# A head's convolution tile accumulated in PSUM between the scores' mask and the mean's sum; early tiles take one GLU group more; gates multiplied in ahead of the variance

## The reference

```python
h = rms_norm(x, norm_g);  z = h @ w_in
(c_glu, c_gate, r_q, r_k, r_v, r_gate, a_q, ...) = split(z)
# convolution branch: 1024 channels, 31 taps along the sequence
v = a * sigmoid(b)                       # a, b = halves of c_glu
y = conv_general_dilated(v, dw, depthwise, width 31) + db
y = silu(layer_norm(y)) * silu(c_gate)
# retention branch: 4 heads, q/k of 256, v of 512
q, k = rotary(q), rotary(k)
o = (q k^T * decay) v                    # both directions
o = (o - mean(o)) * rsqrt(var(o) + EPS)  # over the head's 512 values
y_ret = (o * silu(r_gate)) @ w_ret_out
...
x = x + (g0 * y_conv + g1 * y_ret + g2 * y_attn) @ w_out
```

## Time and profile before

| what | value |
|---|---|
| median of 3 runs | 3453.9 us (3451.58 to 3454.66) |
| the profiled execution | 3454.71 us, its span 3452.9 us |
| TensorE busy | 3243.9 us, 94% of the span |
| DVE, POOL, ACT busy | 1696.8, 1330.2, 1130.9 us |
| mean granted TensorE clock | 0.971 |

### The profile page before, as it was taken

One profiled execution on the slowest core, in us unless ns is written; L12 is line 12 of the kernel. 1 busy time (PEld: TensorE's weight loads), 2 busy tenths in 40 slices (PEclk: granted clock), 3 DMA queues, 4 the chain that ended last, 5 costly groups with the idle time before them and its releaser, 6 DMA issues.

```text
span 3452.9 us, 42695 instructions
## 1 busy us (share of the span) xinstructions
PE 3243.9 (94%) x14040; PEld 2532.5 (73%) x14040; DVE 1696.8 (49%) x2508; ACT 1130.9 (33%) x1623; POOL 1330.2 (39%) x966
## 2 busy tenths in 40 slices
PE   7989999899999898999989999998999999999998
PEld 5866776667888686776766778885787787688885
DVE  4945854765343376745857544245654051341113
ACT  3232232255242222332323653223544332222222
POOL 3433443311555343433433134452334344244542
PEclk9999999999999999999999999999999999999999
DMA  4211222210322322211221022222112223222222
GB/s 150 92 62 61 73 73 66 69 37 25 116 98 92 106 92 73 68 67 61 73 74 55 30 81 92 97 98 79 64 64 73 91 81 102 67 90 97 94 97 73
DMA packets 73172, 272.07 MB, mean 79 GB/s; under 512 B 8128, under 2 KB 9152, under 8 KB 72384
## 3 DMA queue, kind: packets, MB, share of 16 engines
q1 hardware_dynamic: 69984, 252.74, 22.2%
q10 hardware_dynamic: 3072, 17.82, 1.4%
HBM read 264.24 MB, written 8.39 MB: 79 GB/s over the span
## 4 chain that ended last, share of the span: by engine, by line
PE 76%; DVE 11%; DVEq 9%; issue 2%; ACT 1%; DMA 0%; ACTq 0%; POOL 0%; SPq 0%; POOLq 0%
PE gem L296 18%; PE gem L298 18%; PE gem L297 18%; DVEq L1269 3%; PE xp L380 3%; PE xp L536 2%; DVE xp L1233 2%; PE xp L372 2%; DVEq L1235 2%; PE gem L499 2%; DVE zlo L1207 1%; PE gem L633 1%; PE gem L634 1%; PE gem L635 1%; PE xp L506 1%
## 5 line engine op out<-in xcount | busy, mean ns | idle before, releaser
L266 POOL TENSOR_TENSOR wlo<-raw,whi 128x512 fp32r<-128x512 f32 x956 | 1329.4, 1412 | 2078.6 <-ACT whi L774 2078.1
L296 PE MATMUL gem<-hhi,whi 128*128 128x512 f32 x2320 | 935.0, 403 | 4.5 <-POOL wlo L266 3.7
L298 PE MATMUL gem<-hhi,wlo 128*128 128x512 f32 x2320 | 905.1, 390 | 0.0
L297 PE MATMUL gem<-hlo,whi 128*128 128x512 f32 x2320 | 904.1, 390 | 0.0
L774 ACT ACTIVATE whi<-raw 128x1024 fp32r<-128x1024 f32 x478 | 504.4, 1056 | 753.5 <-PE gem L298 651.7
L296 PEld LDWEIGHTS gem<-hhi,whi 128*128 128x128 f32 x2320 | 436.3, 188 | 109.1 <-issue 17.5
L297 PEld LDWEIGHTS gem<-hlo,whi 128*128 128x128 f32 x2320 | 436.5, 188 | 104.5 <-issue 16.3
L298 PEld LDWEIGHTS gem<-hhi,wlo 128*128 128x128 f32 x2320 | 436.1, 188 | 92.1
L296 PE MATMUL gem<-zhi,whi 128*128 128x512 f32 x1008 | 405.6, 402 | 77.0 <-DVE yr L1337 59.9
L297 PE MATMUL gem<-zlo,whi 128*128 128x512 f32 x1008 | 401.9, 399 | 0.0
L298 PE MATMUL gem<-zhi,wlo 128*128 128x512 f32 x1008 | 401.0, 398 | 0.0
(11 more groups left out here) (228 smaller groups left out, 3383.8 us busy)
## 6 DMA issues: line engine op xcount, KB each, us to landing
raw<-in_slabs SPq DMA_DIRECT2D x478, 512.0 KB, 3.4
U<-xsave ACTq DMA_DIRECT2D x2, 2048.0 KB, 7.9
xsave<-U ACTq DMA_DIRECT2D x2, 2048.0 KB, 7.5
U<-in_x ACTq DMA_DIRECT2D x1, 2048.0 KB, 9.5
out_y<-yr SPq DMA_DIRECT2D x8, 256.0 KB, 2.0
tab<-in_tab_ret ACTq DMA_DIRECT2D x2, 512.0 KB, 8.0
tab<-in_tab_att ACTq DMA_DIRECT2D x2, 512.0 KB, 3.6
tab<-in_tab_hg ACTq DMA_DIRECT2D x1, 512.0 KB, 8.0
```

Of the source, the lines that this page charges most:

```text
L266: part = pool.tensor_tensor(wlo[:, k % 4, c], raw[:, k % 2, c], whi[:, k % 4, c].bitcast(f32), O.subtract)
L296: pe.matmul(o, wh, hi, start=(n == 0), stop=False)
L297: pe.matmul(o, wh, lo, start=False, stop=False)
L298: mm = pe.matmul(o, wl, hi, start=False, stop=(n == len(terms) - 1))
```

## The change

- The head's convolution tile accumulates in the `xp` banks 2 and 3, from which the scores have just been read. Its first 27 taps (`HEAD_CUT`) stand right behind `mask_scores`, ahead of the `sum4` that waits for the head's output; the last 4 and the final sum stand behind the `sum4` of the squares. Nothing of it is left in `add_out`.
- `pv` has two banks instead of four (`v % 2`): its third and fourth product wait until ACT has read the first and the second (`o_ready`). The transposes into banks 2 and 3 wait for the end of the convolution (`conv_done`).
- The gate's products (`gate_products`) are taken out of `gated` and stand behind the `sum4` of the squares. `gated` splits two tiles at a time.
- The early convolution has 8 pieces of 12 taps, one behind each GLU product from the first on, instead of 6 of 13; the last tap writes to SBUF directly, which saves a copy. The `memset` of `yr` moves ahead of the GLU.

```diff
-CUTS = (17, 21, 25, 28, TAPS)
-EARLY, EARLY_GLU, EARLY_PIECE = 4, 6, 13
+EARLY, EARLY_GLU, EARLY_PIECE = 4, 8, 12
+HEAD_CUT = 27
...
                 def pv(hd, v):
                     if v == 0:
                         pe.wait_ge(st_ready, L * 16 + hd * 4 + 4)
+                    if v >= 2:
+                        pe.wait_ge(o_ready, L * 16 + hd * 4 + (v - 1))
                     for j in range(4):
-                        mm = pe.matmul(xp[:, v, :], VT[:, j, v * P:(v + 1) * P], ST[:, j, :],
+                        mm = pe.matmul(xp[:, v % 2, :], VT[:, j, v * P:(v + 1) * P], ST[:, j, :],
...
                     for k in range(4, 8):
                         hslab(Gn, k, un)
+                        if k == 5:
+                            pe.wait_ge(conv_done, L * 4 + hd + 1)
...
+                dve.memset(yr[:, :, :], 0.0)
                 for it in range(4):
...
-                        if it:
-                            n = (it * 2 + k // 2 - 2) * EARLY_PIECE
-                            early_conv(n, n + EARLY_PIECE)
+                        n = (it * 2 + k // 2) * EARLY_PIECE
+                        early_conv(n, n + EARLY_PIECE)
                 early_conv(EARLY_GLU * EARLY_PIECE, EARLY * TAPS)
-                dve.memset(yr[:, :, :], 0.0)
...
                     for n in range(first, end):
-                        a, v = TT[:, n % 2, :], cv[:, i, n:n + T]
+                        acc, v, w = xp[:, 2 + n % 2, :], cv[:, i, n:n + T], DW[:, n:n + 1]
                         if n < 2:
-                            ts(a, v, DW[:, n:n + 1], None, O.mult)
+                            ts(acc, v, w, None, O.mult)
                         else:
-                            stt(a, v, DW[:, n:n + 1], a, O.mult, O.add)
+                            stt(acc if n < TAPS - 1 else TT[:, 0, :], v, w, acc, O.mult, O.add)
...
                     mask_scores(hd)
+                    conv(hd + EARLY, 0, HEAD_CUT)
                     sum4(OT, o_ready, L * 16 + hd * 4 + 4, osum)
                     center(hd)
                     sum4(ST, osq, L * 16 + hd * 4 + 4, ossq)
-                    dve.drain()
+                    gate_products(hd)
+                    conv(hd + EARLY, HEAD_CUT, TAPS)
                     dve.wait_ge(ovar, L * 4 + hd + 1)
                     rope(G + 1, u + 1, 0)
                     gated(hd)
                     rope(G + 1, u + 1, 1)
                     dve.drain()
-                    conv(hd + EARLY, 0, CUTS[0])
-                    add_out(G + 3, u + 3, hd + EARLY)
+                    add_out(G + 3, u + 3)
```

More of the change, by code:

```diff
@@ L195, in build @@
         vt_done, vt_ready, score_done, st_ready = (sem(n) for n in ("vt_done", "vt_ready", "score_done", "st_ready"))
-        pv_done, o_ready = sem("pv_done"), sem("o_ready")
+        pv_done, o_ready, conv_done = sem("pv_done"), sem("o_ready"), sem("conv_done")
         osum, omean, ocent, osq, ossq, ovar, orstd = (sem(n) for n in (
@@ L438, in layer @@
                 hslab(G + 1, 3, u + 1)
+                pe.wait_ge(conv_done, L * 4 + 4)
                 for v in range(2):
@@ L851, in o_read @@
                     act.wait_ge(pv_done, L * 16 + hd * 4 + (v + 1))
-                    act.activation(OT[:, v, :], xp[:, v, :], A.Copy).then_inc(o_ready, 1)
+                    act.activation(OT[:, v, :], xp[:, v % 2, :], A.Copy).then_inc(o_ready, 1)
                 def gates(G, hd):
@@ L1232, in early_conv @@
                             else:
-                                stt(acc, v, w, acc, O.mult, O.add)
+                                stt(acc if n < TAPS - 1 else TT[:, 0, :], v, w, acc, O.mult, O.add)
                             if n % 2:
@@ L1237, in early_conv @@
                             dve.drain()
-                            dve.tensor_copy(TT[:, 0, :], xp[:, 0, :])
-                            dve.drain()
                             stt(cv[:, i, PAD:PAD + T], xp[:, 1, :], vec[:, C_CB + i:C_CB + i + 1], TT[:, 0, :], O.add, O.add)
+                dve.memset(yr[:, :, :], 0.0)
                 for it in range(4):
@@ L1248, in layer, with conv @@
                             .then_inc(evac[k], 1)
-                        if it:
-                            n = (it * 2 + k // 2 - 2) * EARLY_PIECE
-                            early_conv(n, n + EARLY_PIECE)
+                        n = (it * 2 + k // 2) * EARLY_PIECE
+                        early_conv(n, n + EARLY_PIECE)
                 early_conv(EARLY_GLU * EARLY_PIECE, EARLY * TAPS)
-                dve.memset(yr[:, :, :], 0.0)
-                def conv(i, first=0, end=TAPS):
+                def conv(i, first, end):
+                    dve.drain()
                     if first == 0:
-                        dve.drain()
                         dve.tensor_copy(DW[:, 0:TAPS], vec[:, bass.ds(i * TAPS + C_DW, TAPS)])
@@ L1271, in conv @@
                         dve.drain()
-                        stt(cv[:, i, PAD:PAD + T], TT[:, 0, :], DW[:, TAPS:TAPS + 1], TT[:, 1, :], O.add, O.add)
+                        stt(cv[:, i, PAD:PAD + T], xp[:, 3, :], DW[:, TAPS:TAPS + 1], TT[:, 0, :], O.add, O.add)\
+                            .then_inc(conv_done, 1)
                         dve.drain()
@@ L1316, in center, with gate_products @@
                         stt(OT[:, v, :], xp[:, 0, :], -1.0 / T, OT[:, v, :], O.mult, O.add).then_inc(ocent, 1)
+                def gate_products(hd):
+                    for v in range(4):
+                        tt(OT[:, v, :], OT[:, v, :], SG[:, v, :], O.mult)
                 def gated(hd):
@@ L1321, in gated, with add_out @@
                     dve.wait_ge(orstd, L * 4 + hd + 1)
[L1322 to L1331, removed]
+                    for v in range(0, 4, 2):
+                        for w in (v, v + 1):
+                            tt(OT[:, w, :], OT[:, w, :], RS, O.mult)
+                        dve.drain()
+                        for w in (v, v + 1):
+                            dve.tensor_copy(zhi[:, w, :], OT[:, w, :])
+                        dve.drain()
+                        for w in (v, v + 1):
+                            tt(zlo[:, w, :], OT[:, w, :], zhi[:, w, :].bitcast(f32), O.subtract).then_inc(z_ready, 1)
+                def add_out(G, u):
                     for k in range(4):
@@ L1337, in add_out @@
                             tt(yr[:, o, :], gem[:, b, :], yr[:, o, :], O.add).then_inc(evac[b], 1)
-                        if i is not None:
-                            conv(i, CUTS[k], CUTS[k + 1])
                 G, u = g0 + QKV0[0], u0 + QKV0[1]
@@ L1368, in layer @@
                 mask_scores(3)
+                conv(EARLY + 3, 0, HEAD_CUT)
                 sum4(OT, o_ready, L * 16 + 16, osum)
@@ L1371, in layer @@
                 sum4(ST, osq, L * 16 + 16, ossq)
+                gate_products(3)
+                conv(EARLY + 3, HEAD_CUT, TAPS)
                 gated(3)
@@ L1383, in layer @@
                 square(0)
-                conv(EARLY + 3, 0, CUTS[0])
-                add_out(G + 2, u + 2, EARLY + 3)
+                add_out(G + 2, u + 2)
                 def a_norm_rope(n):
```

## The result

The changed kernel takes 3379.68 us (median of 4 runs, 3376.34 to 3380.46) against 3454.28 for the kernel before on the same chip: a ratio of 0.9783, 95% interval 0.9766 to 0.9800. That is 74.6 us less, where 69.4 were forecast. The profiled execution took 3380.46 us with a span of 3378.7, so 74.2 of the 3452.9 before are gone; its mean granted clock is 0.980.

What follows compares the result with a forecast made beforehand. TensorE, busy 94% of the span, was taken as the bound. The terms 78.7 + 27.3 + 5.0 - 22.4 - 19.2 = 69.4 us gained gave 3454.7 - 69.4 = 3385.3, stated as 3385 us, range 3356 to 3412.

Steps and rivals of the forecast that it cites:

- `add_out`, 78.7: TensorE's eight waits for `add_out`, in four heads of two layers, all go: 59.9 us plus 18.8 of low clock.
- The early tiles, 27.3: Early convolution tiles finish in time, so both first-head rope waits go: 22.9 us plus 4.4 of low clock.
- The convolution fits: In each head, 27 taps with weight copies take 23.4 us in 29.0 us of room and cost nothing.
- My dearer price: Taps at 1.002 us, as with SBUF accumulators: a head's 27 would take 28 us and still fit.
- The new `pv` waits, 22.4: The third `pv` waits for ACT's read behind a table load: 2.8 us in each of eight heads, 22.4 lost.
- The fourth rival: ACT's `pv` read comes 1.4 us later behind the table load; eight heads lose 11 us: 3398 us. Chance 0.02.
- The clock behind them, 19.2: Lower granted clock behind the eight new `pv` waits: 2.4 us a head, 19.2 lost, bounds nothing and 4.4 each.
- Head 3, 5.0: TensorE's wait for `zlo` in head 3 shrinks: 2.5 us gained per layer, 5 in all, bounds nothing and 14.
- this rival: The convolution doesn't fit at 1.76 us a tap; TensorE waits 19.4 us at each mean: 3559 us. Chance 0.04.
- my 8.7: Wait in us per head, at the mean, at which the 69.4 us gain would be used up.
- The rope wait: Rival: early tiles finish late and TensorE waits for the first head's rope again, 27.3 us: 3412. Chance 0.05.
- the stall: Rival: with `add_out` prompt, a 3.7 us wait for POOL's weights comes in each head, 30 us: 3415. Chance 0.06.

Runs made afterwards that it cites:

- the doubled taps: The changed kernel with the first 20 taps of each head's convolution tile done twice; 3439.61 us, ratio 0.9953 to the kernel before.

## Why the prediction was right

The time, the direction and the mechanism came out as forecast, by the forecast's own steps; two terms were mis-sized, in opposite directions, so that the time came out closer than its terms.

**`add_out`, 78.7.** The waits, 59.9 us, are gone entirely, as said. The 18.8 of clock were read from the kernel before and not measured by themselves after.

**The early tiles, 27.3.** Shown alone at 24.7 to 26.3, so 1 to 2.6 too much. Also the margin was smaller than I had it. DVE's rows in the first layer, which answer to the earlier trace rows: the `memset`, the last early tap, the end of the second rope, and the first masked score; then PE's first scores.

```profile
47.82 3.47 DVE L1245 MEMSET yr<- 128x4096 f32 x1 [0.80 <-issue]
...
154.13 0.75 DVE L1243 SCALAR_TENSOR_TENSOR cv<-xp,vec,U 128x512 f32<-128x512 f32 x1
...
162.47 1.78 DVE L1295 TENSOR_TENSOR U<-U,tab 128x512 f32<-128x512 f32 x1
...
166.63 0.69 DVE L1299 TENSOR_TENSOR U<-U 128x512 f32<-128x512 f32 x1
...
174.90 0.69 DVE L1305 TENSOR_TENSOR U<-xp,U 128x512 f32<-128x512 f32 x1 [5.17 <-PE xp L372]
...
172.99 3.60 PE L372 MATMUL xp<-U 128*128 128x512 f32 x8
```

The tiles ended at 154.9 (152.5 forecast), the ropes at 167.3 (161): I priced a rope at 4 us, but it has rows of 1.6 to 1.78 among those of 0.68 and takes about 6. TensorE comes to the scores at 172.99, without a wait, so 5.7 us were left; I had counted 10.5 (161 against 171.5).

**The convolution fits.** A tap took 0.75 us, a pair with its gap 1.58 instead of my 1.67 (I had left out that two overlap a little). The 27 took 21.3 us, and 9 to 10.6 us were to spare rather than 5.6. DVE waited 7.05 for the head's output in head 1, where I had said 4. My dearer price for the taps, 28 us, left out the gaps: 27 x 1.002 + 13.5 x 0.17 + 0.9 is 30.2, over the room of 29.0, so it was wrong that they fit by either price. It didn't come to that: with SBUF accumulators at this place, head 1's 27 taps took 22.8 us (299.12 to 321.89).

**The new `pv` waits, 22.4.** They are 20.8: 2.60 each instead of 2.8. The fourth rival, a read that comes late behind the table load, is excluded: the read starts 0.02 us behind the load's end. The drain of about 1380 ns that the Trainium skill, page "ScalarE: Activation LUTs", section "What ACT_TABLE_LOAD costs", adds to a load does not show in this trace; its 1283 ns for the load agree with the row's 1.28 us.

**The clock behind them, 19.2: mis-sized.** It cost half. The windows of 6 us behind the `pv` waits of the changed kernel, the four of layer 1, then the four of layer 2:

```profile
205.85:211.85 6.00, 6.00 (x14) 2.77 (x15) 2.13 (x3) 1.03 (x2) 0.00 (x0) 1.00 0.01 3
320.71:326.71 6.00, 6.00 (x11) 2.71 (x12) 2.12 (x3) 1.03 (x2) 0.00 (x0) 0.74 0.00 0
437.08:443.08 6.00, 6.00 (x7) 2.52 (x8) 2.13 (x3) 0.43 (x1) 0.00 (x0) 0.50 0.00 0
555.01:561.01 6.00, 6.00 (x10) 2.60 (x11) 0.78 (x2) 1.00 (x2) 0.00 (x0) 0.72 0.00 0
1339.54:1345.54 6.00, 6.00 (x14) 2.76 (x15) 2.14 (x3) 1.03 (x2) 0.00 (x0) 1.00 0.01 3
1454.39:1460.39 6.00, 6.00 (x14) 2.77 (x15) 2.13 (x3) 1.03 (x2) 0.00 (x0) 1.00 0.00 0
1569.25:1575.25 6.00, 6.00 (x10) 2.58 (x11) 2.13 (x3) 1.00 (x2) 0.00 (x0) 0.72 0.00 0
1685.79:1691.79 6.00, 6.00 (x10) 2.65 (x11) 0.78 (x2) 1.03 (x2) 0.00 (x0) 0.72 0.00 0
```

Three of the eight lose nothing, four lose 1.6 to 1.7 us, one 3.0: 9.6 in all. I had taken a value between the rows of a shorter and a longer wait for each; the rows fall near both ends and in the middle, for waits of one length.

**Head 3, 5.0: mis-sized.** It gained 0.6 us of waiting: 9.4 against twice 5.02. DVE in head 3, first layer, and POOL beside it:

```profile
576.32 5.78 DVE L1324 TENSOR_TENSOR U<-U 128x512 f32<-128x512 f32 x4
...
586.22 1.88 DVE L1332 TENSOR_TENSOR U<-U 128x512 f32<-128x512 f32 x2
...
589.01 1.29 DVE L1338 TENSOR_TENSOR zlo<-U,zhi 128x512 fp32r<-128x512 f32 x2
...
594.40 1.29 DVE L1338 TENSOR_TENSOR zlo<-U,zhi 128x512 fp32r<-128x512 f32 x2
...
574.39 6.55 POOL L266 TENSOR_TENSOR wlo<-raw,whi 128x512 fp32r<-128x512 f32 x4 [5.74 <-ACT whi L779]
```

The four products stand beside POOL's splits and take 5.78 us, where I had 4.7. The first `zlo` comes sooner, but the second pair's comes 5.4 us behind it, and TensorE, which has run six matmuls on the first pair by 591.4, waits for that one: 0.98 and then 3.74 us instead of 5.02 once. My reading that the first half slab needs all four tiles was right, and should have set the term. The clock gave nothing back either: over the 6 us behind the long wait it is 0.57 in layer 1 and 0.72 in layer 2, against 0.57 and 0.71 before.

**The sum**, with the measured terms where there are any, is 78.7 + 24.7 to 26.3 + 0.6 - 20.8 - 9.6 = 73.6 to 75.2, against 74.2 between the spans. With my 27.3 for the early tiles it would be 76.2. These 2 us too much lie in the clock: the waits among the terms (59.9 + 22.9 + 0.6 - 20.8 = 62.6) nearly make the 63.4 of waiting that went away, but the clock terms (18.8 + 4.4 - 9.6 = 13.6) are 2.8 more than the 10.8 by which TensorE's busy time fell. The four runs of the changed kernel differ by more than that among themselves. My 69.4 came near in part by luck: 11.2 us too much for `pv` and its clock stood against 4.4 too much for head 3.

**The rivals.** No mean waits in the changed kernel; the doubled taps show that this rival's mechanism is real, and that by the estimate above the gain is used up at waits of 7.5 us a head, not at my 8.7, which left out the clock. The rope wait didn't return, and the stall did not come back under another name: POOL's wait is one of 3.7 us, as before.

## What to carry to other kernels

When work is moved into an idle stretch, ask first what else works in that stretch: here the same taps in the same SBUF tiles became nearly as cheap as in PSUM, since in the head shown only one pair ahead of the sum met POOL's work, and the move to other banks brought only a new wait. When banks are halved, look where the reader's read stands in its engine's list: three lines of order on ACT were worth about 30 us. The two versions of the change that only take away the `pv` wait, at 3349.9 us, beat the change and the kernel before (3.0% under it).

## What the runs showed of the hardware

What two SBUF inputs cost depends in these rows on POOL: a pair of taps takes 1.41 us beside an idle POOL and 3.43 when it meets two of POOL's splits (304.86 to 307.80). Values between occur too: in the kernel before, the pairs at 403.07 and 405.66 share two splits (403.22 to 406.61) and take 2.42 and 2.16. With the accumulator in PSUM, the changed kernel's pair at 308.02 stands beside POOL's splits as well and takes 1.41:

```profile
308.02 1.41 DVE L1269 SCALAR_TENSOR_TENSOR xp<-cv,sm,xp 128x512 f32<-128x512 f32 x2 [0.17 <-issue]
...
307.45 2.50 POOL L266 TENSOR_TENSOR wlo<-raw,whi 128x512 fp32r<-128x512 f32 x2 [6.38 <-ACT whi L779]
```

The Trainium skill, page "SBUF — State Buffer", section "Who interferes with whom", says that a DVE instruction with two SBUF inputs contends with a GpSimd instruction that reads SBUF; these rows agree with it. A mean such as 1002 or 845 ns mostly says how often POOL worked beside the tap.

The granted clock behind TensorE's waits of one length, 2.60 us, was 1.00, 0.72 to 0.74, or 0.50 over the next 6 us. With the same waits in the kernel before with two `pv` banks alone it was 1.00 once and 0.72 seven times, so the length alone doesn't tell the loss. What decides it is not shown here.
